# Projecting a memory's keys and values later, and two modulation blocks as matmuls with moving weights

## What is computed

```python
mod = jax.nn.silu(c) @ ada_w[layer] + ada_b[layer]          # c: one row of 1024; ada_w: 1024 x 6144
shift1, scale1, gate1, shift2, scale2, gate2 = ...split(mod, 6)
u = rms_norm(h, norm1_g[layer]) * (1 + scale1) + shift1
z = u @ w_in[layer]                                          # everything of block 1 starts from it
...
mixed = (sigmoid(m_a) * y_a + sigmoid(m_b) * y_b) @ w_out[layer]
h = h + gate1 * mixed
u2 = rms_norm(h, norm2_g[layer]) * (1 + scale2) + shift2
...
# second block, memory attention; mem is an input of 256 x 1024
kv = (rmsnorm(mem, mem_norm) @ w_kv).reshape(B, M, MEM_HEADS, MEM_HEAD_DIM)
k = rmsnorm(kv[..., :MEM_WIDTH]..., k_norm); v = kv[..., MEM_WIDTH:]...
```

## Time and profile before

| | us |
|---|---|
| median of 3 runs | 1184.56 |
| lowest and highest | 1183.53, 1186.32 |
| the profiled execution | 1182.56 |
| its span in the trace | 1180.8 |
| granted TensorE clock, mean over the span | 0.977 |
| PE busy | 1112.4 (94%) |
| DVE, ACT, POOL busy | 694.5 (59%), 587.6 (50%), 438.7 (37%) |

### The profile page before, as it was taken

How to read it: one execution, slowest core, us unless ns; L and a number is a source line. 1 busy time by engine, 2 the same in 40 slices (tenths; PEclk the granted TensorE clock), 3 DMA queues, 4 the chain that set the end, 5 groups by cost and what they waited for, 6 DMA issues and landing times.

```text
span 1180.8 us, 21915 instructions
## 1 busy us (share of the span) xinstructions
PE 1112.4 (94%) x8532; PEld 1071.7 (91%) x8532; DVE 694.5 (59%) x1120; ACT 587.6 (50%) x1033; POOL 438.7 (37%) x236
## 2 busy tenths in 40 slices
PE   4789999899889999999999999999999887999999
PEld 3679989888889999999999998999899887999998
DVE  6455848986758952336777523565776774444421
ACT  3445536554455654545444545688545345444432
POOL 5440111311444444543444453433233234444443
PEclk8889999999989999999999999999999998999999
DMA  9546988322445555555555554444333343555553
GB/s 363 210 142 221 351 311 274 129 70 92 156 130 179 183 186 185 178 178 179 182 186 186 179 181 145 157 144 162 125 125 126 125 144 124 185 189 179 181 184 119
DMA packets 58260, 208.04 MB, mean 176 GB/s; under 512 B 6799, under 2 KB 8207, under 8 KB 58040
## 3 DMA queue, kind: packets, MB, share of 16 engines
q1 hardware_dynamic: 51784, 183.64, 46.9%
q0 software_dynamic: 6384, 23.09, 5.5%
HBM read 205.64 MB, written 1.06 MB: 175 GB/s over the span
## 4 chain that ended last, share of the span: by engine, by line
PE 82%; DVE 9%; ACT 3%; DMA 3%; issue 2%; POOL 1%; SPq 1%; DVEq 0%; ACTq 0%; POOLq 0%
PE bank L607 81%; DMA ring<-in_stream 3%; DVE ring_rounded L1594 1%; POOL ring_rounded L1131 1%; ACT rounded_rounded L1206 1%; PE bank L858 1%; DVE wide L1839 1%; ACT wide L1381 1%; DVE stats L1834 1%; DVE shared L2106 1%; DVE wide_rounded L1868 0%; DVE ada_acc L1671 0%; DVE shared_rounded L1868 0%; SPq L562 0%; DVE wide L1810 0%
## 5 line engine op out<-in xcount | busy, mean ns | idle before, releaser
L1131 POOL TENSOR_TENSOR ring_rounded<-ring,rounded_rounded 128x1024 fp32r<-128x1024 f32 x154 | 385.0, 2500 | 594.9 <-ACT rounded_rounded L1206 594.9
L607 PE MATMUL bank<-u_rounded,rounded_rounded 128*128 128x256 f32 x1528 | 440.9, 289 | 7.7 <-ACT u_rounded L1263 3.9
L607 PE MATMUL bank<-u_rounded,ring_rounded 128*128 128x256 f32 x1528 | 434.5, 285 | 0.0
L607 PE MATMUL bank<-u_lo_rounded,rounded_rounded 128*128 128x256 f32 x1528 | 429.7, 285 | 0.0
L1206 ACT ACTIVATE rounded_rounded<-ring 128x1024 fp32r<-128x1024 f32 x326 | 340.9, 1053 | 171.6 <-PE bank L607 144.1
L1594 DVE TENSOR_TENSOR ring_rounded<-ring,rounded_rounded 128x1024 fp32r<-128x1024 f32 x172 | 257.1, 1496 | 223.2 <-ACT rounded_rounded L1206 222.7
L607 PEld LDWEIGHTS bank<-u_rounded,rounded_rounded 128*128 128x128 f32 x1528 | 295.7, 194 | 12.6 <-issue 11.1
L607 PEld LDWEIGHTS bank<-u_rounded,ring_rounded 128*128 128x128 f32 x1528 | 295.7, 194 | 0.1
L607 PEld LDWEIGHTS bank<-u_lo_rounded,rounded_rounded 128*128 128x128 f32 x1528 | 293.2, 193 | 0.9
L607 PE MATMUL bank<-shared_rounded,rounded_rounded 128*128 128x256 f32 x992 | 258.0, 287 | 2.8 <-DVE wide L1881 2.6
L607 PE MATMUL bank<-wide_rounded,rounded_rounded 128*128 128x256 f32 x864 | 234.6, 287 | 17.7 <-ACT wide_rounded L1255 5.5
(11 more groups left out here) (272 smaller groups left out, 1161.8 us busy)
## 6 DMA issues: line engine op xcount, KB each, us to landing
ring<-in_stream SPq DMA_DIRECT2D x334, 512.0 KB, 3.3
ada_ring<-in_ada POOLq DMA_DIRECT2D x33, 512.0 KB, 5.1
wide<-in_mem_t SPq DMA_DIRECT2D x2, 512.0 KB, 6.1
shared<-in_ada POOLq DMA_DIRECT2D x2, 512.0 KB, 10.1
ada_ring<-in_ada SPq DMA_DIRECT2D x2, 512.0 KB, 14.0
x<-in_x_t SPq DMA_DIRECT2D x1, 1024.0 KB, 14.5
wide<-in_ada POOLq DMA_DIRECT2D x2, 512.0 KB, 21.6
wide<-in_ada SPq DMA_DIRECT2D x2, 512.0 KB, 21.3
```

The costliest lines, as they stand in the source:

```text
L607: return nc.tensor.matmul(out, lhs, rhs, start=start, stop=stop, skip_group_check=True)
L1131: pool.tensor_tensor(R(w), w, R(slot_round(q)), ALU.subtract).then_inc(slot_split_by_pool, 1)
```

## The change

The memory's work leaves the start. Its norm is computed among the input projections of block 1: SP loads the memory after the early modulation, ACT squares it, POOL adds the squares up, and PE sums them with one matmul after `kb1`. The high and the low part (1 MB each) are stored to a scratch tensor in DRAM by POOL's queue and loaded back before the merging. `mem_k0` to `mem_k3` are projected after `up_sb0`, `up_sb2`, `up_sb4` and `up_sb6`, and `mem_v0/1` after `mix7`, with `x1_ss` in their middle.

The start now goes: sum of squares of x; then the 16 early chunks of ada_w on PE, as the moving operand of 32 plain fp32 matmuls of 512 columns, against a stationary operand in which c is repeated over 128 columns (`c_spread`). Each of four banks then holds half of a block, the same on every partition; DVE multiplies by the identity and sums (`ada_diagonal`), which leaves the column on its partition. The shift comes in two halves. `vsw` takes the low parts of u one by one. DVE now splits all slots before `mb0`. The bias matmul stands behind `ga`.

The core of the diff:

```diff
-ADA_ARRIVAL = (1, 3, 5, 7, 9, 0, 11, 13, 2, 15, 4, 6, 8, 10, 12, 14)
-EARLY_SLOTS = 10
+ADA_BEFORE_MEM, ADA_OVER_MEM = 21, 29
+ADA_BY_POOL_QUEUE = ((1, 0), (1, 1), (1, 2), (1, 3), (1, 4), (0, 0), (0, 1), (0, 2), (0, 3))
+ADA_BY_SP_QUEUE = ((1, 5), (1, 6), (1, 7), (0, 4), (0, 5), (0, 6), (0, 7))
+ADA_ARRIVAL = ((1, 0), (1, 1), (1, 5), (1, 2), (1, 6), (1, 3), (1, 7), (1, 4),
+               (0, 4), (0, 0), (0, 1), (0, 5), (0, 6), (0, 2), (0, 7), (0, 3))
...
-    for b in range(4):
-        stationary("mem_w_kv_2", span(b * P), full)
-    moving("mem_w_kv_2", 512, 512, KD)
...
+        if m % 2 == 0:
+            stationary("mem_w_kv_2", span(m // 2 * P), full)
     for m in range(KD):
         stationary("w_out", span(m * P), full)
+    moving("mem_w_kv_2", 512, 512, KD)
...
+        mem_hi, mem_lo = shared[:, 4:12, :], bias
...
+        c_spread = flat(turned[:, 1, :, :]).rearrange("p (k c) -> p k c", c=P)
...
-            for half, name in ((slice(0, 4), "mem"), (slice(4, 8), "mem_end")):
-                sp.dma_start(mem_n[:, half, :], mem_t[:, half, :]).then_inc(loaded[name], 16)
+            for half, name in ((slice(0, 4), "x"), (slice(4, 8), "x_end")):
+                sp.dma_start(x[:, half, :], x_t[:, half, :]).then_inc(loaded[name], 16)
+            for part_and_chunk in ADA_BY_SP_QUEUE[:4]:
+                load_ada_early(*part_and_chunk)
+            sp.dma_start(mats[:, MAT["ident"], :], mats_d[:, MAT["ident"], :]).then_inc(ident_loaded, 16)
             load(0, 0)
-            load_ada_shift(0)
-            sp.dma_start(x[:, :, :], x_t).then_inc(loaded["x"], 16)
+            for part_and_chunk in ADA_BY_SP_QUEUE[4:]:
+                load_ada_early(*part_and_chunk)
             for r in range(1, 4):
-                load_ada_shift(2 * r - 1)
                 load(r, r)
-                load_ada_shift(2 * r)
-            load_ada_shift(7)
+            sp.dma_start(mats[:, 2:, :], mats_d[:, 2:, :]).then_inc(loaded["mats"], 16)
+            for r in range(4, RING):
+                load(r, r)
             sp.dma_start(buckets, buckets_d).then_inc(loaded["bias_in"], 16)
             sp.dma_start(table[:, :], table_d).then_inc(loaded["bias_in"], 16)
-            for r in range(4, RING):
-                load(r, r)
-            sp.dma_start(mats[:, 1:, :], mats_d[:, 1:, :]).then_inc(loaded["mats"], 16)
...
+            full(sp, "ada0b")
+            for half, name in ((slice(0, 4), "mem"), (slice(4, 8), "mem_end")):
+                sp.dma_start(mem_n[:, half, :], mem_t[:, half, :]).then_inc(loaded[name], 16)
...
-            sum_row("mem_ss", ROW_MEM, row_squares)
-            mem_parts, u_parts, hidden_parts = (mem_n, mem_n_lo), (u, u_lo), (hidden, hidden_lo)
-            project_first("mem_k0", mem_parts, ROW_MEM)
-            project("mem_k1", KD, mem_parts)
-            sum_squares("mem_k0", "ones")
+            u_parts, hidden_parts, mem_parts = (u, u_lo), (hidden, hidden_lo), (mem_hi, mem_lo)
+            pe.wait_ge(ones_ready, 2)
             sum_row("x_ss", ROW_X, merged)
-            project("mem_k2", KD, mem_parts)
-            sum_squares("mem_k1", "ones")
-            project("mem_k3", KD, mem_parts)
-            sum_squares("mem_k2", "ones")
+            pe.wait_ge(c_spread_ready, 1)
+            met = [0, 0]
+            for j, k in ADA_ARRIVAL:
+                pe.wait_ge(ada_early_full[j, k], 16)
+                for half, c in enumerate("ab"):
+                    name = f"ada{j}{c}"
+                    ps = bank(name) if met[j] else claim(name)
+                    ins = mm(ps[:, :], c_spread[:, k, :], ada_early[j, k][:, half * 512:(half + 1) * 512], met[j] == 0, met[j] == KD - 1)
+                    if met[j] == KD - 1:
+                        done(ins, name)
+                met[j] += 1
+            project_tokens(["vsw0", "vsw1"], KD, u_parts, 256, ready=lambda i: pe.wait_ge(u_ready, ROW_X * KD + i + 1))
+            project_tokens(["vsb0", "vsb1"], KD, u_parts, 512)
+            project("ga", KD, u_parts)
             pe.wait_ge(loaded["bias_in"], 32)
             done(mm(claim("bias")[0:8, 0:512], table[:, :], buckets[:, :], True, True), "bias")
-            sum_squares("mem_k3", "ones")
-            project_tokens(["mem_v0", "mem_v1"], KD, mem_parts, 512, ada_first_parts)
-            pe.wait_ge(loaded["mats"], 16)
-            pe.wait_ge(u_ready, (ROW_X + 1) * KD)
-            project_tokens(["vsw0", "vsw1"], KD, u_parts, 256)
-            project_tokens(["vsb0", "vsb1"], KD, u_parts, 512)
-            project("ga", KD, u_parts)
...
+                if b == 1:
+                    ps = claim("mem_ss")
+                    pe.wait_ge(row_gathered, 1)
+                    done(mm(ps[:, 0:T], mat("ones"), mem_squares[:, 0, :], True, True), "mem_ss")
...
+                if m % 2:
+                    sum_squares(f"mem_k{m // 2}", "ones")
                 project(f"up_sb{m}", 4, (attn_b, attn_b_lo1), (lambda i: evacuated(pe, f"sbo{i}")) if m == 0 else None)
+                if m == 0:
+                    pe.wait_ge(loaded["mem_back"], 32)
+                if m % 2 == 0:
+                    project(f"mem_k{m // 2}", KD, mem_parts)
...
-            sum_gathered("x1_ss", ROW_1)
+            project_tokens(["mem_v0", "mem_v1"], KD, mem_parts, 512, lambda: sum_gathered("x1_ss", ROW_1))
...
+            for j, k in ADA_BY_POOL_QUEUE:
+                pool.dma_start(ada_early[j, k], ada[j * KD + k]).then_inc(ada_early_full[j, k], 16)
...
+            pool.wait_ge(row_squares_ready, (ROW_MEM + 1) * KD)
+            for n in (4, 2, 1):
+                ins = pool.tensor_tensor(mem_squares[:, 0:n, :], mem_squares[:, 0:n, :], mem_squares[:, n:2 * n, :], ALU.add)
+                if n > 1:
+                    at["gathered"] += 1
+                    ins.then_inc(row_gathering, 1)
+                    pool.wait_ge(row_gathering, at["gathered"])
+            ins.then_inc(row_gathered, 1)
+            for n in range(ADA_BEFORE_MEM, ADA_OVER_MEM):
+                load_ada(n)
...
+            pool.wait_ge(u_rounded, (ROW_MEM + 1) * KD)
+            pool.dma_start(mem_parts_kept[0], R(mem_n)).then_inc(mem_stored, 16)
+            pool.wait_ge(u_ready, (ROW_MEM + 1) * KD)
+            pool.dma_start(mem_parts_kept[1], R(mem_n_lo)).then_inc(mem_stored, 16)
+            for n in range(ADA_OVER_MEM, 48):
+                load_ada(n)
...
+            evacuated(pool, "sbz7")
+            pool.wait_ge(mem_stored, 32)
+            pool.dma_start(R(mem_hi), mem_parts_kept[0]).then_inc(loaded["mem_back"], 16)
+            split_slots_until("mb5")
+            pool.wait_ge(logits_ready, 8)
+            pool.dma_start(R(mem_lo), mem_parts_kept[1]).then_inc(loaded["mem_back"], 16)
...
+            act.wait_ge(mem_stored, 32)
...
+            def ada_diagonal(j, half):
+                name = f"ada{j}{'ab'[half]}"
+                full(dve, name)
+                kept = ada_acc[:, half, 0:512].rearrange("p (i c) -> p i c", c=P)
+                free(v.tensor_tensor(kept, bank(name)[:, :].rearrange("p (i c) -> p i c", c=P),
+                                     mat("ident").unsqueeze(1).to_broadcast([P, 4, P]), ALU.mult), name)
+                evacuated(dve, name)
+                step(v.tensor_reduce(out=mod[:, j * 8 + 4 * half:j * 8 + 4 * half + 4], in_=kept, axis=AX.X, op=ALU.add))
+            for half in range(2):
+                ada_diagonal(1, half)
+            scale = mod[:, 8:16]
+            step(v.scalar_tensor_tensor(out=scale, in0=scale, scalar=1.0, in1=ada_bias(1), op0=ALU.add, op1=ALU.add))
+            step(v.tensor_tensor(scale, scale, gains("norm1_g"), ALU.mult))
+            dve.wait_ge(row_rinv_ready, ROW_X + 1)
+            for i in range(KD):
+                v.scalar_tensor_tensor(out=u_lo[:, i, :], in0=x[:, i, :], scalar=mod[:, 8 + i:9 + i], in1=row_rinv[:, :],
+                                       op0=ALU.mult, op1=ALU.mult).then_inc(u_normed, 1)
+            ahead("x_ss", 2)
+            def shift_half(half):
+                ada_diagonal(0, half)
+                at = slice(4 * half, 4 * half + 4)
+                v.tensor_tensor(mod[:, at], mod[:, at], ada_bias(0)[:, at], ALU.add).then_inc(shift_ready, 1)
+                dve.wait_ge(shift_ready, half + 1)
+            shift_half(0)
+            for i in range(KD):
+                if i == 2:
+                    shift_half(1)
+                dve.wait_ge(u_rounded, ROW_X * KD + i + 1)
+                v.scalar_tensor_tensor(out=R(u_lo[:, i, :]), in0=u_lo[:, i, :], scalar=mod[:, i:i + 1], in1=R(u[:, i, :]),
+                                       op0=ALU.add, op1=ALU.subtract).then_inc(u_ready, 1)
...
+            norm_row(mem_n, mem_n_lo, mem_n, gains("mem_norm_2"), ROW_MEM, None, lambda: ahead("qb0"))
...
+                    normalise(f"mem_k{m // 2}", [mem_k[:, m // 2, :]], "mem_k_norm_2")
...
+            ahead("mem_v0", 1)
+            norm_row(u, u_lo, x, mod[:, 32:40], ROW_1, mod[:, 24:32], lambda: ahead("mem_v0", 3))
```

198 lines of the change are left out of this document (95 added, 103 removed).

## The result

The changed kernel took 1176.55 us (median of 4 runs, 1175.22 to 1177.52), against 1184.49 for the kernel before (4 runs, 1183.53 to 1186.32). The ratio is 0.9931, with a 95% interval of 0.9917 to 0.9944: 7.9 us faster. The forecast was 17.0 us faster. The direction was right, and the time lies inside the range of 1158 to 1179, but less than half of the forecast gain came. The profiled execution took 1176.05, its span 1174.3, so 6.5 us less than the span before. Beside the runs of the experiments the kernel before was run again each time, with medians of 1183.57 to 1184.32, so that medians of different experiments can be compared to within about 1 us (the intervals reach some 2 us to either side). One of e10's six executions took 2185.54 us, which no trace explains, and is counted as slow (without it e10's median is 1169.51 instead of 1169.76).

A forecast was written before the change was run, and what follows sets the result against it. PE, busy in 94% of the span, was taken as the bound. Terms -38.1 + 1.3 + 10.2 + 5.6 + 4 = -17.0 took 1182.56 to 1165.6, or 1167.5 us against the median 1184.56; range 1158 to 1179.

The forecast's parts named there:

- The start: From the start to vsb: without the memory's work, vsb starts near 48.6 instead of 86.66, -38.1 us.
- The sums in the stream: Bias matmul (0.9) and the memory's one sum (0.44) now stand in PE's dense stream, +1.3 us.
- The keys: Four mem_k products and sums, 13.2 us, fill 3.0 of PE's 3.97 us of waits for DVE: +10.2 us.
- The values: From mix7 to w1_1: mem_v takes 10.9 us and partly hides the norm of x, +5.6 us.
- The stores: Storing the memory's two parts, 2.1 MB, in a stretch where transfers fill the DMA engines: +4 us.
- rival C: More waiting in the dense part, from DVE's added work or a clock fall at the values: about 1176, chance 0.20.
- B: Slower than before: PE runs the 32 matmuls at the start at 1.2 GHz, +28.2 us, 1195.7, chance 0.07.
- The prediction's last sign: From w1_1 to the end, over 2 us of difference from 833.1 means something other than the terms is at work.
- E: Early chunks come late and PE idles between them, the opening still bound by transfers: 1176 and more, chance 0.05.

The follow-up runs named there:

- e10: The changed kernel with POOL's mask eight products later and the one slot beside the low parts before w1_1 split by DVE, not POOL: median 1169.76 us.
- e7: The changed kernel with the 16 early chunks multiplied and added up by DVE, PE only summing over the partitions: median 1177.10 us.
- e8: The changed kernel with useless matmuls on PE before cmp_turn_k, cmp_turn_v and ga_turn, where it waited: median 1172.61 us.
- e6: The changed kernel with useless matmuls on PE in its wait for the low parts before w1_1: median 1172.09 us.
- f2: The changed kernel with the edits of e10 and e8 together: median 1167.97 us, ratio 0.9877 to the kernel before.

## Why the prediction was right or wrong

- **The start (-38.1, measured -37.4)** was right step by step: 32 matmuls of 0.86 us (0.883 in the forecast) between 12.35 and 39.97, at a clock of 1.00; the chunks came ahead of PE; the chain of identity product (0.69), reduction (0.69), shift and low part ended at 42.10 (41.7). But e7 shows that its reason was only half a reason. With DVE adding up the chunks, `vsb` starts at 50.0. The gain is from taking the memory away; the new form of the modulation is worth 0.8 us at the start by the traces, which is less than its scatter. That the first trace had `vsb` within 0.7 us of the forecast was partly luck: in five of fourteen the clock made it 1.7 to 3.1 us later than forecast.
- **The sums in the stream (+1.3)** measured +1.1 and 0.4.
- **The keys (+10.2, measured +8.9)**: all four of PE's waits for DVE there were filled, the end at +9.2 that I had named. No wait for L1951 (L1881 before) is left.
- **The values (+5.6, measured +8.7)** failed in one step: "the low parts take 3.25". I took their time from a stretch in which POOL was quiet, and didn't ask what POOL does beside them in the new place, although had shown 2.63 instead of 0.42 and I used it for the keys. Without POOL beside them (e10) the stretch is 17.2 where the prediction had 17.0.
- **The stores (+4)** failed: the traffic of a saturated stretch was charged in full to PE. Removing it gained nothing, doubling it cost 1.1 to 2.3, near noise. The two errors on this side, 4 us here and 1.3 at the keys, were luck: they made up for part of what was missing elsewhere. The statement that no store stands in the trace was wrong as well, though none of this size does: the output goes out in eight of 128 KB.
- **The dense stretch to ada2** was given no cost, and rival C had named the place and the memory's norm: 2.8 us, of which 0.8 is the wait for DVE, stretched by POOL's additions, and 1.5 (1.1 to 4.1) the wait for a split behind the memory's norm. What C didn't have is that the norm starts late because DVE waits 1.8 to 4.7 us for chunks of ada_w.
- **The clock** was the step that was missing: the forecast put nothing at it outside the rivals B and C. 1.9 us from ada3 to ada4 and 2.1 behind the MLP's first product are half clock behind waits (e8, e6), and so are the 1.4 of the attention and the 2.8 at the end, by where the traces have it. I let the stretches without new instructions stand at the length of one trace of the kernel before. The prediction's last sign, more than 2 us of difference behind `w1_1`, did come: 1174.3 - 336.5 is 837.8, against 833.1.
- **What adds up, and what doesn't.** Between forecast and trace lie 10.6 us: 3.1 at the values, 2.8 before ada2, 2.9 from ada3 to ada4, 2.1 behind the MLP's first product and 0.9 at the start, less 4 for the stores and 1.3 for the keys, together 6.5; and 4.2 of low clock in the attention and at the end. Between forecast and median lie 9.1, 1.5 less, since the traced execution of before was 2.0 us faster than its median and that of after 0.5. What made the others slower isn't in a trace. But each execution's mean granted clock is on record, and the time goes with it: of the kernel before, beside f2, 1178.99 us at 0.981 and 1188.34 at 0.970.
- **Rivals.** B didn't happen at the start. E didn't either: the chunks were in time. C, with 0.20 and 1176, is the rival that came out, at 1176.55; of its causes the clock carried 8.2 us by the traces, at four places, where I had named one.

## What to carry to other kernels

When work moves, take the durations of its steps from a stretch in which the same neighbours run beside it: DVE's steps took about twice as long beside POOL's here. In this kernel, bound by PE, a wait cost itself and at some places 1 to 3 us of half clock behind it, so look at the clock behind waits before looking for bytes; filling them with matmuls into a spare bank, or better giving PE's supplier a quiet stretch, got it back. Where stretches with the same instructions differ between two traces, compare where the clock was low before looking for a cause in the change. And when a change has two parts, price each alone: here one of them bought nothing that can be told from scatter.

## What the runs showed of the hardware that I had not expected

Two waits of 0.4 and 0.8 us with little work of PE around them, and a third of 1.2 in it, went with a granted clock of 0.50 from 140 to 147, while the single wait in a dense stretch ahead of ada2, of 1.1 to 4.1 us (1.53 at 113.15), was followed by none in nine of twelve traces, and by half clock in the three with 2.16, 2.76 and 4.07. The same wait of 2.2 us at 832 was followed by half clock in the changed kernel (0.50 in the window 834 to 836) and by 1.00 in the kernel before. The length of a stretch with the same instructions follows from where the clock is low: five traces with the same four places agree within 0.1 us over 263. At the start of each span the profile gives a clock of 1.00, but the first steps of PE stand 0.43 us apart (until about 10 in both kernels), twice the 0.22 that follow, so this 1.00 is not to be trusted. And three additions of POOL of 6.4 us made DVE's step of 1.28 take 2.90.
